# Index scores: the low part of the keys gets 64 rows of zeros, so that both products of a pair have 128 rows of weights

## What is computed

```python
dots = jnp.einsum('bqhe,bke->bqhk', qi, ki).astype(F32)          # 4 heads of 64 elements, keys shared
score = jnp.einsum('bqh,bqhk->bqk', wi.astype(F32), jax.nn.relu(dots))
admissible = (kpos[None, :] // CHUNK) <= (qpos[:, None] // CHUNK)
score = jnp.where(admissible, score, NEG_INF)
_, sel = lax.top_k(score, topk)
```

## Time and profile before

| | us |
|---|---|
| median of 3 runs | 4718.31 (4712.97 to 4719.27) |
| the profiled execution's own time | 4715.49 |
| its span in the trace | 4713.7 |
| TensorE busy (share of the span) | 4020.4 (85%) |
| VectorE busy | 2415.4 (51%) |
| ScalarE busy | 1552.2 (33%) |
| GpSimd busy | 673.0 (14%) |
| mean granted TensorE clock | 0.902 of full speed |
| first matmul of `index_scores` to the end of its last instruction | 2518.7 to 2754.3 |

### The profile page before, as it was taken

One profiled execution on the slowest core, in us unless ns is written; L12 is line 12 of the kernel. 1 busy time (PEld: TensorE's weight loads), 2 busy tenths in 40 slices (PEclk: granted clock), 3 DMA queues, 4 the chain that ended last, 5 costly groups with the idle time before them and its releaser, 6 DMA issues. The chain is left out here.

```text
span 4713.7 us, 52421 instructions
## 1 busy us (share of the span) xinstructions
PE 4020.4 (85%) x18001; PEld 2724.5 (58%) x18001; DVE 2415.4 (51%) x5162; ACT 1552.2 (33%) x2330; POOL 673.0 (14%) x406
## 2 busy tenths in 40 slices
PE   5999999978869999969897997789667488888798
PEld 3789889956646565648654443334344344555476
DVE  6211111177764454423203579999655677777622
ACT  3110001033423334333203468871133233333433
POOL 3100000021211111114100000000121432111043
PEclk9999999989979999989996578899788689999899
DMA  5222112144332322134312011011311311000143
GB/s 179 63 73 72 65 70 77 56 99 101 94 75 59 73 68 65 29 108 161 110 46 52 12 52 45 31 47 60 105 47 48 79 37 31 22 23 5 70 146 132
DMA packets 222647, 328.50 MB, mean 70 GB/s; under 512 B 22240, under 2 KB 129176, under 8 KB 221040
## 3 DMA queue, kind: packets, MB, share of 16 engines
q1 hardware_dynamic: 162768, 216.87, 16.3%
q10 hardware_dynamic: 54432, 91.91, 5.3%
q0 software_dynamic: 5216, 16.70, 1.7%
HBM read 214.42 MB, written 110.99 MB: 69 GB/s over the span
## 5 line engine op out<-in xcount | busy, mean ns | idle before, releaser
L2299 DVE TENSOR_SCALAR_CACHE_REDUCE cd_junk<-score,cd_thr 128x384 bf16<-128x384 f32 (+7 forms) x340 | 397.8, 1237 | 0.1
L1102 DVE TENSOR_REDUCE attB_mx<-attB_p_s 128x1 f32<-128x512 f32 (+2 forms) x360 | 211.3, 609 | 323.9 <-PE attB_p_s L949 207.5
L497 DVE COPY ab_stage<-ab_pA 128x256 f32<-128x256 f32 (+1 forms) x108 | 56.5, 523 | 600.3 <-PE ab_pA L466 576.2
L2339 ACT ACTIVATE cd_scratch<-score,cd_less 128x1664 bf16<-128x1664 f32 (+4 forms) x160 | 303.2, 1895 | 71.9 <-DVE cd_less L2318 66.4
L369 PE MATMUL cd_pA<-hT_cd,cd_W 128*128 128x512 f32 (+1 forms) x640 | 263.8, 577 | 72.9 <-ACT cd_stage L2445 62.2
L464 PE MATMUL ab_pA<-ab_W_hi,h_hi 128*128 128x256 f32 x1088 | 309.0, 284 | 3.2 <-PE ab_pA L466 3.1
L465 PE MATMUL ab_pA<-ab_W_lo,h_hi 128*128 128x256 f32 x1088 | 307.9, 283 | 0.0
L466 PE MATMUL ab_pA<-ab_W_hi,h_lo 128*128 128x256 f32 x1088 | 307.8, 283 | 0.0
L1575 PE MATMUL attD_p_o<-attD_pt,attD_v 128*65 128x512 f32 x548 | 296.8, 624 | 0.1
L1014 PE MATMUL attB_p_o<-attB_pt,attB_v 128*65 128x512 f32 (+3 forms) x656 | 286.2, 525 | 0.0
L495 ACT ACTIVATE ab_stage<-ab_pA 128x256 f32<-128x256 f32 (+1 forms) x108 | 50.0, 463 | 697.2 <-PE ab_pA L466 666.7
(11 more groups left out here) (376 smaller groups left out, 9447.3 us busy)
## 6 DMA issues: line engine op xcount, KB each, us to landing
t_qg<-cd_stage ACTq DMA_DIRECT2D x74, 256.0 KB, 2.0
ab_W_raw<-in_w_ab SPq DMA_DIRECT2D x17, 1024.0 KB, 5.8
mix_o<-t_o SPq DMA_DIRECT2D x34, 512.0 KB, 4.3
t_q<-ab_stage ACTq DMA_DIRECT2D x40, 256.0 KB, 2.0
t_k<-ab_stage ACTq DMA_DIRECT2D x40, 256.0 KB, 2.0
attA_raw<-t_k SPq DMA_DIRECT2D x16, 640.0 KB, 7.6
attA_raw<-t_q SPq DMA_DIRECT2D x16, 640.0 KB, 12.6
attB_raw<-t_k SPq DMA_DIRECT2D x16, 640.0 KB, 7.6
```

What stands on the lines that cost most here:

```text
L1102: nc.vector.tensor_reduce(out, src, AX.X, ALU.max).then_inc(s_free, 1)
L2299: nc.vector.tensor_scalar(junk[n % 2][:, 0:w], sc[n][:], T[:, n:n + 1], None, op, ALU.add, accum_out=cnt[:, n:n + 1]).then_inc(counted, 1)
L2339: nc.scalar.activation(scratch[:, 0:w], sc[n][:], ACT.Sign, bias=less[:, k:k + 1], accum_out=cnt[:, n:n + 1]).then_inc(signed, 1)
```

## The change

The tiles of the low part of the keys get all 128 rows. GpSimd fills their rows 64 to 127 with zeros at the start of the block, and TensorE waits for that before its first product. The second product reads all 128 rows of `q2` and of the low part of the keys; the added rows multiply the rest of the queries by zero. VectorE writes rows 0 to 63 of the low part as before.

```diff
-        kp_lo, ks_lo = sb("kp_lo", [HD, ROWS], F32R), sb("ks_lo", [HD, SEQ], F32R)
+        kp_lo, ks_lo = sb("kp_lo", [P, ROWS], F32R), sb("ks_lo", [P, SEQ], F32R)
...
             @block.tensor
             def _(pe):
+                pe.wait_ge(cleared, 2)
...
                     nc.tensor.matmul(out, q2[n % 2][:, h, :], kh[:, ks], start=True, stop=False)
-                    nc.tensor.matmul(out, q2[n % 2][0:HD, h, :], kl[:, ks], start=False, stop=True).then_inc(dots, 1)
+                    nc.tensor.matmul(out, q2[n % 2][:, h, :], kl[:, ks], start=False, stop=True).then_inc(dots, 1)
+
+            @block.gpsimd
+            def _(pool):
+                nc.gpsimd.memset(kp_lo[HD:P, :].bitcast(F32), 0.0).then_inc(cleared, 1)
+                nc.gpsimd.memset(ks_lo[HD:P, :].bitcast(F32), 0.0).then_inc(cleared, 1)
...
-                    nc.vector.tensor_tensor(lo[:], k_raw[0:HD, 0:w], hi[0:HD].bitcast(F32), ALU.subtract
+                    nc.vector.tensor_tensor(lo[0:HD], k_raw[0:HD, 0:w], hi[0:HD].bitcast(F32), ALU.subtract
```

More of the change, by code:

```diff
@@ L2131, in index_scores @@
         loaded, dots, relud, summed, masked = (sem(n) for n in ("loaded", "dots", "relud", "summed", "masked"))
-        k_in, k_rounded, k_split, q_rounded, q_split = (sem(n) for n in (
-            "k_in", "k_rounded", "k_split", "q_rounded", "q_split"))
+        k_in, k_rounded, k_split, q_rounded, q_split, cleared = (sem(n) for n in (
+            "k_in", "k_rounded", "k_split", "q_rounded", "q_split", "cleared"))
         q_in = [sem(f"q_in{k}") for k in range(2)]
```

## The result

| | before | changed |
|---|---|---|
| median of the runs, us | 4718.79 (4712.97 to 4723.36, 4 runs) | 4602.41 (4597.78 to 4607.85, 4 runs) |
| profiled execution, own time and span, us | 4715.49, 4713.7 | 4597.78, 4596.0 |
| mean granted clock | 0.902 | 0.923 |

The changed kernel takes 0.9755 of the time before, 95% interval 0.9739 to 0.9771: 116 us less. Forecast were 105 us less and 4613, with a range of 4603 to 4632. In the changed kernel the two products are lines 2189 and 2190, the ReLU 2220, the split of the queries 2228, the first-head multiplication 2251, the addition 2254 and the mask 2259.

What follows compares the result with a forecast made beforehand. PE was taken to bound the index-score block at 210.3 us; afterwards DVE's 104 us plus 1 us gives 105, a gain of 105 us. Profiled 4715.5 becomes 4610.5, plus 2.8 for the median: 4613 us, range 4603 to 4632.

Steps and rivals of the forecast that it cites:

- The bound before: Index-score block: PE alone sets the time, 209.8 us counted against 210.3 in the trace.
- What is removed: Alternating 64- and 128-row products keep weight loads from hiding, 0.293 us per product; PE falls to 120.4 us, or 67 at 2.4 GHz.
- Rival 2: Index-score products: loads wait for something else, such as both reading tile q2; no difference, 4718 us; chance 0.06.
- rival 4: Index-score products: each load waits for the full array to empty, 0.07 us each; 24 us slower, 4742; chance 0.02.
- What bounds it then: Index-score block after the change: DVE bounds at 104.2 us, ahead of PE's 67 at full clock and ACT's 100.5 at most.
- duration less 0.04: DVE operations in a stream: each costs its record less 0.04 us overlap, so 0.711 us per addition of 512 columns.
- the additional 1 us for waits: Index-score block: 1 us added to DVE's 104 for moments at half clock and DVE waiting on ACT.
- The clock: PE in the index-score block: granted clock rises to 2.4 GHz, as in attention A and B; over 0.9 from about 2545.
- rival 1: Index-score block: clock stays at 1.2 GHz, PE bounds at 120.4 us; gain 90 us, 4628; chance 0.16, low or mostly low.
- What is added: Block start: two GpSimd memsets, 4 to 9.7 us together, taken as 4, hidden under PE's 19.97 us wait; cost 0.
- What comes late next: Query transfers in the short query blocks: 8.9 us available against 7.7 needed; cost 0, dear end 5 us.
- Rival 3: Short query blocks stall on late queries: up to 5 us of the gain, 4618; no separate chance, inside DVE-bound 0.76.

Runs made afterwards that it cites:

- the 66-row run: Changed kernel with the low part of the keys and the second product at 66 rows instead of 128: 4604.29 us, ratio 0.9762 to the kernel before.
- the run with the added work alone: Changed kernel with padded tiles, memsets and TensorE's wait kept, but the second product reading 64 rows as before: 4715.85 us, ratio 0.9998.
- the first comparison: Changed kernel with the zero-padded low keys, timed beside the kernel before: 4602.41 us against 4718.79.
- the second: Changed kernel timed once more, unaltered, beside the kernel before and the version with wide additions: 4605.38 us, ratio 0.9762 to before.
- the other run: Changed kernel with both the split of the queries and the mask moved from VectorE to GpSimd: 4602.71 us, ratio 0.9761 to before.

## Why the prediction came out as it did

**The bound before.** Right. Halved additions left 210.6 us unchanged, and the count of 209.8 from columns and 0.293 us per product matched the 210.3 of the trace.

**What is removed.** Right, and now shown by itself: the price of 0.293 us belongs to a change between 64 and 128 rows. One change for two products cost half (165.4 us, forecast 165), none cost nothing (120.3 for 120.4), and 66 rows cured it. Rival 2, no effect, and rival 4, slower, are out; both products of the 66-row run still read the same tile q2. The rule that the prediction cites from the Trainium skill (TensorE: Matmul & The Clock Gate, Part 3), that loads overlap only with other row groups, is contradicted by the loads above that run beside products on the same rows. The rule that it cites from the Trainium skill (TensorEngine Tiling (Array Packing), Key Properties), that changing the tiling mode drains TensorE, agrees with where the cost came and where it didn't. That it is such a drain no trace shows.

**What bounds it then.** The bound was named rightly; this is the step whose size was off. The term "duration less 0.04" for an operation in a stream was taken from a piece of six in which narrow and wide ones alternate. Where six of 512 columns follow each other, one costs 0.66 us and not 0.711, an overlap of 0.09. Over 90 such additions this is 4.6 us, nearly all of the difference between the reckoned 104.2 us of DVE and the 99.3 of the stage; the additional 1 us for waits was not needed. The prediction had priced this case, an overlap of 0.1 us, as the low end of its range; that the total fell just below that end is the 5 us of scatter. The forecast of 2649 for the end of the last mask looks exact (2649.3 to 2649.55), and this is luck: the stage began 6.5 us late and was 6 us shorter than forecast.

**The clock.** The forecast of 2.4 GHz came out (a granted clock of 0.98 over the stage), but its reason was too wide. "A stream without gaps has not stayed low elsewhere" is wrong as a rule: with 64 or 66 rows in both products a stream without gaps stayed at 0.50 for the 120 us of the stage. The outcome hung on the first product's 128 rows, which the prediction did not weigh, so that here it was right by luck in part. The price of rival 1, 120.4 us for the stage, is what those two kernels measured.

**What is added.** Right: memsets of 3.7 us against the 4 taken, over 13 us ahead of the first product, and the run with the added work alone is at 0.9998 of the time before.

**What comes late next.** Right for the queries: behind the third mask ScalarE has no wait for their transfers in the trace, and 99.3 us leaves no room for a stall of 5. Rival 3 did not happen.

**The rest.** The prediction said that later stages would not change by more than a few us. Attention C was 7.5 us shorter, but it varies by 9 from run to run, without a cause in this change that the traces show. The 116.4 us of the first comparison are 5 more than the stage's 111.3; the 111.0 of the second are not.

## What to carry to other kernels

Look at the distance between starts of successive matmuls and compare it with columns divided by clock: a constant remainder of a load's length, with idle time ahead of each load that nothing explains, says that loads don't run ahead. If products of 64 rows alternate with products of 128, pad the short ones (66 rows were enough here) or order them so that equal ones meet (this gave 45 us of the 111). After such a gain count the next engine in a stream of its own kind and width, and ask apart from that whether the clock will rise.

## What the runs showed of the hardware

- A change between products of 64 and of 128 rows costs 0.29 us at 1.2 GHz, in both directions (0.72 us between products of 512 columns). With 64 and 64, 66 and 66, 128 and 66 or 128 and 128 rows the distance is 0.43 us, the columns alone.
- The granted clock stayed at 0.50 for the 120 us of a stream without gaps whose products all had 64 rows, or all 66. It rose to 1.00 when every other one had 128, with either 66 or 128 in the rest.
- GpSimd's memset of 64 x 2176 took 1.9 us and hid under the wait for keys; its subtraction of 64 x 512, 1.3 to 1.8 us, stretched VectorE's mask beside it from 0.29 to 1.27 us and, in the other run, its multiplication of 512 columns from 0.48 to 0.75 on average.
